# Attention with the transposes three heads behind, VectorE normalising first, and negated logits

## The reference

```
logits = where(valid, (q @ k.T) * SCALE + bias, NEG)
m = max(max(logits), sink)                  # sink: first 16 heads alone
e = exp(logits - m)
p = e / (sum(e) + exp(sink - m))
y = p @ v                                   # 256 x 64 per head
yn = rms(y[:, :1024]) * ga ++ rms(y[:, 1024:]) * gb
x = x + g1 * (yn @ w_o)
x = x + g2 * experts(rms(x) * (1 + sc2) + sh2)
```

## Time and profile before

| | us |
|---|---|
| median of 3 runs | 1583.15 |
| lowest, highest | 1582.28, 1590.99 |
| profiled execution | 1584.59 |
| its span | 1582.8 |
| PE busy, share | 1361.7, 86% |
| DVE busy, share | 652.2, 41% |
| ACT busy, share | 138.7, 9% |
| first scores of the attention | 307.78 |
| last square sum ends | about 402.9 |

### The profile page before, as it was taken

One profiled execution on the slowest core, in us unless ns is written; L12 is line 12 of the kernel. 1 busy time (PEld: TensorE's weight loads), 2 busy tenths in 40 slices (PEclk: granted clock), 3 DMA queues, 4 the chain that ended last, 5 costly groups with the idle time before them and its releaser, 6 DMA issues.

```text
span 1582.8 us, 14568 instructions
## 1 busy us (share of the span) xinstructions
PE 1361.7 (86%) x5720; PEld 690.4 (44%) x5720; DVE 652.2 (41%) x984; ACT 138.7 (9%) x390; POOL 48.2 (3%) x60
## 2 busy tenths in 40 slices
PE   2799998898898468998988988988988988988985
PEld 2678777566687355332332322332332332332321
DVE  4557676556575632224224224223223223233234
ACT  2110000146200011000000000000000000000001
POOL 0000000000100000000000000000000000000000
PEclk9899999959999789999999999999999999999998
DMA  9999999814498860999999999999999999999992
GB/s 334 397 361 401 394 362 359 323 69 160 141 392 324 314 266 27 376 425 428 424 426 429 424 425 430 424 425 429 424 425 429 424 425 430 424 425 430 424 424 85
DMA packets 96295, 572.10 MB, mean 361 GB/s; under 512 B 6048, under 2 KB 28752, under 8 KB 54400
## 3 DMA queue, kind: packets, MB, share of 16 engines
q1 hardware_dynamic: 94256, 567.64, 87.8%
q0 software_dynamic: 2000, 3.95, 0.9%
HBM read 569.38 MB, written 2.18 MB: 361 GB/s over the span
## 4 chain that ended last, share of the span: by engine, by line
PE 65%; DMA 24%; DVE 6%; issue 3%; ACT 1%; SPq 1%; DVEq 0%; POOL 0%; POOLq 0%; ACTq 0%
PE PS L1298 20%; DMA ring<-in_w_up 18%; PE PS L1319 10%; PE PS L1144 9%; PE PS L1278 8%; PE PS L1223 5%; PE PS L1149 3%; DMA ring<-in_w_ada 3%; DMA ring<-in_w_o 2%; PE PS L1260 2%; DVE W L761 2%; DVE W L1029 1%; PE PS L1094 1%; PE PS L1174 1%; PE PS L1194 1%
## 5 line engine op out<-in xcount | busy, mean ns | idle before, releaser
L1298 PE MATMUL PS<-ring,W 128*64 128x512 f32 x1024 | 239.0, 624 | 38.3 <-DMA ring<-in_w_up 38.1
L1319 PE MATMUL PS<-ring,W 128*64 128x512 f32 x1024 | 233.6, 610 | 27.4 <-DVE W L1029 17.7
L1298 PE MATMUL PS<-ring,gysq 128*64 128x512 f32 x1024 | 229.4, 604 | 15.9 <-DMA ring<-in_w_up 12.4
L1144 PE MATMUL PS<-r,ring 128*128 128x256 f32 x768 | 171.2, 386 | 9.2 <-DVE r L771 7.5
L1007 DVE TENSOR_TENSOR r<-r,PS 128x512 f32<-128x512 f32 x128 | 88.0, 688 | 200.5 <-PE PS L1278 200.5
L1298 PEld LDWEIGHTS PS<-ring,W 128*64 128x64 f32 x1024 | 81.2, 144 | 190.4 <-issue 190.4
L1144 PEld LDWEIGHTS PS<-r,ring 128*128 128x128 f32 x768 | 148.5, 194 | 32.6 <-DVE r L771 8.3
L761 DVE SCALAR_TENSOR_TENSOR W<-ring,sm,W 128x2048 f32<-128x2048 f32 x60 | 140.8, 2347 | 40.4 <-DMA ring<-in_w_ada 37.2
L1012 DVE TENSOR_SCALAR W<-W 128x256 f32<-128x256 f32 x32 | 22.0, 689 | 311.5 <-ACT W L660 311.5
L1298 PEld LDWEIGHTS PS<-ring,gysq 128*64 128x64 f32 x1024 | 78.6, 139 | 164.6 <-issue 164.6
L1319 PEld LDWEIGHTS PS<-ring,W 128*64 128x64 f32 x1024 | 76.2, 140 | 163.6 <-issue 144.0
(11 more groups left out here) (207 smaller groups left out, 737.3 us busy)
## 6 DMA issues: line engine op xcount, KB each, us to landing
ring<-in_w_gate SPq DMA_DIRECT2D x64, 2048.0 KB, 25.2
ring<-in_w_up SPq DMA_DIRECT2D x64, 2048.0 KB, 27.0
ring<-in_w_down SPq DMA_DIRECT2D x64, 2048.0 KB, 26.2
ring<-in_w_ada SPq DMA_DIRECT2D x32, 2048.0 KB, 15.4
ring<-in_w_qkv SPq DMA_DIRECT2D x17, 2048.0 KB, 16.7
ring<-in_w_ada SPq DMA_DIRECT2D x32, 1024.0 KB, 14.3
ring<-in_w_o SPq DMA_DIRECT2D x8, 2048.0 KB, 14.7
ring<-u_scr SPq DMA_DIRECT2D x2, 2048.0 KB, 19.8
```

Source lines behind the costliest of these rows:

```text
L1144: last = mm(ps[:, sub * T:(sub + 1) * T], w[:, t, (2 * b + sub) * P:(2 * b + sub + 1) * P], hT[:, QT * q + t, :], start=(t == 0), stop=(t ...
L1298: last = mm(PS[64 * j:64 * j + 64, i % 2, :].rearrange("p (m n) -> p m n", m=2), hE[i % 2][:, k], w[:, :, t, 256 * j:256 * j + 256], start ...
L1319: last = mm(PS[64 * q:64 * q + 64, 4 + i2, :], hidT[:, b, 64 * j:64 * j + 64], w[:, b, 512 * ch:512 * ch + 512], start=(j + b == 0), stop= ...
```

## The change

Logits are kept negated: q is scaled by -SCALE and the bias table is negated, so that the row minimum of the negated logits is the negated maximum that Exp needs as its bias, and Exp runs with scale -1. L840 goes. DVE normalises head h-2 first, then evicts y, and takes logits(h) last. Transposes run three heads behind, values and everything behind them two steps later; a fifth buffer for logits is added. The squares are no longer summed over blocks on PE: ACT writes the first block's square of each half into `ysq`, POOL adds each further one, and two products with ones follow after the loop. The waits for the modulation row move: ACT's behind head 3, PE's behind the loop, and POOL does its adds between the write of row SH2 and its read back.

```diff
-    line[rel_bucket(dist), np.arange(UL)] = (dist >= 0)
+    line[rel_bucket(dist), np.arange(UL)] = -1.0 * (dist >= 0)
...
+        ysq = gy
+        Ls = [L[:, i] for i in range(4)] + [W[:, 2816:2816 + 384]]
+        NL = len(Ls)
...
+            def add_square(b):                                   # POOL
+                i, n = divmod(b, KT // 2)
+                if n:
+                    pool.wait_ge(sq_ok, b + 1)
+                    total = ysq[:, i * T:(i + 1) * T]
+                    nc.gpsimd.tensor_tensor(total, total, sq[:, b % 2 * T:(b % 2 + 1) * T], ALU.add).then_inc(ysq_ok, 1)
+                    pool.wait_ge(ysq_ok, b - i)
...
                 pool.dma_start(m_scr[pt_].rearrange("(q n) -> q n", q=4), rows).then_inc(mod_out, 16)
+                if pt_ == SH2:
+                    for h in range(NH + 7):
+                        if h >= 8 and h % 2 == 0:
+                            add_square((h - 8) // 2)
                 pool.wait_ge(mod_out, 16 * (i + 1))
...
             def exps(h):                                         # ACT
-                act.wait_ge(nm_ok, h + 1)
-                A.activation(L[:, h % 4, 0:T], L[:, h % 4, 0:T], ACT.Exp, bias=nmx[:, h, 0:1],
+                act.wait_ge(lg_ok, h + 1)
+                Lh = Ls[h % NL]
+                A.activation(Lh[:, 0:T], Lh[:, 0:T], ACT.Exp, bias=nmx[:, h, 0:1], scale=-1.0,
                              accum_out=psum_[:, h, 0:1])
...
             def squares(b):
                 act.wait_ge(y_ok, b + 1)
-                if b >= 2:
-                    act.wait_ge(yss_ps, b - 1)
-                A.activation(sq[:, b % 2 * T:(b % 2 + 1) * T], yT[:, b, :], ACT.Square).then_inc(sq_ok, 1)
-            act.wait_ge(mod_out, 16 * 2)
+                i, n = divmod(b, KT // 2)
+                if n == 0:
+                    A.activation(ysq[:, i * T:(i + 1) * T], yT[:, b, :], ACT.Square).then_inc(sq_ok, 1)
+                else:
+                    if b >= 3:
+                        act.wait_ge(ysq_ok, b - 2 - (b - 2) // (KT // 2))
+                    A.activation(sq[:, b % 2 * T:(b % 2 + 1) * T], yT[:, b, :], ACT.Square).then_inc(sq_ok, 1)
             act.wait_ge(small_in, 32)
-            for h in range(NH + 4):
+            for h in range(NH + 7):
                 if h < NH:
                     exps(h)
-                if 2 <= h < NH + 2:
-                    pt_evac(h - 2)
-                if h >= 5 and h % 2 == 1:
-                    squares((h - 5) // 2)
+                if h == 3:
+                    act.wait_ge(mod_out, 16 * 2)
+                if 3 <= h < NH + 3:
+                    pt_evac(h - 3)
+                if h >= 8 and h % 2 == 0:
+                    squares((h - 8) // 2)
...
+            link(V.tensor_scalar(nsink, sink, -1.0, None, ALU.mult))      # DVE
             def logits(h):
                 dve.wait_ge(s_ps, h + 1)
-                if h >= 4:
-                    dve.wait_ge(pt_ps, h - 3)
+                if h >= NL:
+                    dve.wait_ge(pt_ps, h - NL + 1)
...
-                dve.wait_ge(lg_ok, h + 1)
-                V.tensor_scalar(nmx[:, h, :], nmx[:, h, :], -1.0, None, ALU.mult).then_inc(nm_ok, 1)
...
-            for h in range(NH + 4):
-                if h < NH:
-                    logits(h)
-                if 1 <= h <= NH:
-                    normalise(h - 1)
-                if h >= 5 and h % 2 == 1:
-                    y_evac((h - 5) // 2)
-            dve.wait_ge(yss_ps, NH // 2)
+            for h in range(NH + 6):
+                if 2 <= h < NH + 2:
+                    normalise(h - 2)
+                if h >= 7 and h % 2 == 1:
+                    y_evac((h - 7) // 2)
+                if h < NH:
+                    logits(h)
+            dve.wait_ge(yss_ps, 2)
...
-            pe.wait_ge(mod_ok, 2)                                # PE
-            for h in range(NH + 5):
+            for h in range(NH + 6):
                 if h < NH:
                     scores(h)
-                if 2 <= h < NH + 2:
-                    transpose_p(h - 2)
-                if 4 <= h < NH + 4 and h % 2 == 0:
-                    values((h - 4) // 2)
+                if 3 <= h < NH + 3:
+                    transpose_p(h - 3)
                 if h >= 6 and h % 2 == 0:
-                    square_sums((h - 6) // 2)
+                    values((h - 6) // 2)
+            pe.wait_ge(mod_ok, 2)
+            for i in range(2):
+                pe.wait_ge(sq_ok, KT // 2 * i + 1)
+                pe.wait_ge(ysq_ok, (KT // 2 - 1) * (i + 1))
+                mm(PS[:, 6 + i, 0:T], ones, ysq[:, i * T:(i + 1) * T], start=True, stop=True).then_inc(yss_ps, 1)
```

More of the change, by code:

```diff
@@ L39 @@
 NEG = -1e30
-LOW = -3.0e38
+HIGH = 3.0e38
 SCALE = 1.0 / math.sqrt(HD)
@@ L102, in constants @@
     line = np.zeros((BUCKETS, 2 * UL), np.float32)
-    line[rel_bucket(dist), np.arange(UL)] = (dist >= 0)
+    line[rel_bucket(dist), np.arange(UL)] = -1.0 * (dist >= 0)
     bad = np.zeros((NH, UL), np.float32)
-    bad[:NHA, (dist < 0) | (dist >= WINDOW)] = NEG
-    bad[NHA:, dist < 0] = NEG
+    bad[:NHA, (dist < 0) | (dist >= WINDOW)] = -NEG
+    bad[NHA:, dist < 0] = -NEG
     line[:, UL:] = bad
@@ L184, in layer_kernel @@
         gy, sq = gysq[:, 0:H * CW], gysq[:, H * CW:H * CW + 2 * T]
+        ysq = gy
         idr = sb("idr", H * P)
-        sm = sb("sm", 608)
+        sm = sb("sm", 624)
         ovi = sb("ovi", 1, I32)
@@ L248, in small @@
             at[0] += n
-            assert at[0] <= 608
+            assert at[0] <= 624
             return sm[:, at[0] - n:at[0]]
@@ L256, in layer_kernel @@
         A1, B1, A2, B2 = small(KT), small(KT), small(KT), small(KT)
-        sink = small(NHA)
+        sink, nsink = small(NHA), small(NHA)
         nmx, psum_, rden = (small(NH * 2).rearrange("p (h t) -> p h t", t=2) for _ in range(3))
@@ L301, in layer_kernel @@
         qkv_ok = sem("qkv_ok")
-        s_ps, lg_ok, nm_ok, p_ok, sum_ok = sem("s_ps"), sem("lg_ok"), sem("nm_ok"), sem("p_ok"), sem("sum_ok")
+        s_ps, lg_ok, p_ok, ysq_ok = sem("s_ps"), sem("lg_ok"), sem("p_ok"), sem("ysq_ok")
         pn_ok, pt_ps, pt_ok, y_ps, y_ok, sq_ok, yss_ps = (sem("pn_ok"), sem("pt_ps"), sem("pt_ok"), sem("y_ps"),
@@ L561, in _ @@
                     if k < 2:
-                        A.activation(query(k, b), backwards(ps), ACT.Copy, scale=SCALE).then_inc(qkv_ok, 1)
+                        A.activation(query(k, b), backwards(ps), ACT.Copy, scale=-SCALE).then_inc(qkv_ok, 1)
                     elif k == 2:
@@ L578, in exps @@
             def exps(h):
-                act.wait_ge(nm_ok, h + 1)
-                A.activation(L[:, h % 4, 0:T], L[:, h % 4, 0:T], ACT.Exp, bias=nmx[:, h, 0:1],
+                act.wait_ge(lg_ok, h + 1)
+                Lh = Ls[h % NL]
+                A.activation(Lh[:, 0:T], Lh[:, 0:T], ACT.Exp, bias=nmx[:, h, 0:1], scale=-1.0,
                              accum_out=psum_[:, h, 0:1])
-                last = A.activation(L[:, h % 4, T:384], L[:, h % 4, T:384], ACT.Exp, bias=nmx[:, h, 1:2],
+                last = A.activation(Lh[:, T:384], Lh[:, T:384], ACT.Exp, bias=nmx[:, h, 1:2], scale=-1.0,
                                     accum_out=psum_[:, h, 1:2])
@@ L770, in add_part @@
                 if k < 2:
-                    V.scalar_tensor_tensor(query(k, b), backwards(ps), SCALE, query(k, b), ALU.mult,
+                    V.scalar_tensor_tensor(query(k, b), backwards(ps), -SCALE, query(k, b), ALU.mult,
                                            ALU.add).then_inc(qkv_ok, 1)
@@ L826, in _ @@
             mod_row(1)
+            dve.wait_ge(small_in, 32)
+            link(V.tensor_scalar(nsink, sink, -1.0, None, ALU.mult))
             def logits(h):
                 dve.wait_ge(s_ps, h + 1)
-                if h >= 4:
-                    dve.wait_ge(pt_ps, h - 3)
+                if h >= NL:
+                    dve.wait_ge(pt_ps, h - NL + 1)
                 B = on_ring(dve, "bias", h // 16).rearrange("p (h k) -> p h k", h=16)[:, h % 16, :]
[L834 to L838, removed]
-                dve.wait_ge(lg_ok, h + 1)
-                V.tensor_scalar(nmx[:, h, :], nmx[:, h, :], -1.0, None, ALU.mult).then_inc(nm_ok, 1)
+                high = nsink[:, h:h + 1] if h < NHA else HIGH
+                Lh = Ls[h % NL]
+                V.tensor_tensor_reduce(out=Lh[:, 0:T], in0=PS[:, h % 2, 0:T], in1=B, scale=1.0, scalar=high,
+                                       op0=ALU.add, op1=ALU.min, accum_out=nmx[:, h, 0:1])
+                V.tensor_tensor_reduce(out=Lh[:, T:384], in0=PS[:, h % 2, T:384], in1=B[:, P:T], scale=1.0,
+                                       scalar=high, op0=ALU.add, op1=ALU.min, accum_out=nmx[:, h, 1:2]).then_inc(lg_ok, 1)
             def normalise(h):
                 dve.wait_ge(p_ok, h + 1)
+                Lh = Ls[h % NL]
                 if h < NHA:
@@ L846, in normalise @@
                 link(V.reciprocal(rden[:, h, :], psum_[:, h, :]))
```

(30 more changed lines are left out.)

## The result

Median of 9 runs: 1591.66 us (1587.77 to 1592.83) against 1583.89 before (1579.11 to 1590.99). The ratio is 1.0047, 95% interval 1.0027 to 1.0066. The profiled execution took 1588.92 (span 1587.1), 4.3 above the profiled one of before; it is the second fastest of the nine.

The account below looks back on a forecast made before the run. Attention was taken as the bound, PE alone at 1.2 GHz and a three-engine round at full clock. Start, loop and tail gave +7.8, tail clock -1.6, w_o -0.3: +5.9, 1589 us as median, range 1571 to 1595.

Parts of the forecast that it names:

- Fall at 311: Start of attention: PE's thin stretch lets the clock fall to 0.50 at 311 us or one step later.
- No rise in the loop: Attention loop: without the full-array square sums PE stays at 1.2 GHz through the whole loop; 59 in 100.
- rival A: Attention: full clock returns at about 322 once PE is filled; L864 at 374, -29, total 1554; 6 in 100.
- Start, -1.8: Start of attention: ACT's wait for m_scr moves behind head 3, so first transposes come 1.8 us earlier, at about 313.2.
- Loop, 94.5 us of PE work, pair 6.30: Attention loop at 1.2 GHz: PE alone sets 6.30 us per pair, 94.5 us left, last values end at 407.7.
- Tail: Last values to L864: 3.0 us instead of 1.7, with POOL's last add; clock returning there gives back 1.6.
- The clock came back in the tail: After scores 31: 7.8 us of dense transposes and values bring the clock back, -1.6 (0 to -2.8).
- the bounds: Tail: POOL's last two-input add takes between 0.26 and 2.1 us, with 0.8 taken.
- w_o, -0.3: Start of w_o after attention: begins at the lower clock again, slow work slightly shorter, -0.3 (-1 to +0.5).
- The total: Whole kernel: terms sum to +5.9, 1590.5 us in the profiled frame, 1589 in that of the median.
- 1.90 us per head: First 16 heads at full clock: DVE's logits, normalise and half an eviction take 1.90, or 3.8 per pair.

Follow-up runs that it names:

- experiment 1: Kernel after, with PE multiplying constants (seven fillers) in its waits in the first seven steps: 1556.33 us, ratio 0.9828.
- experiment 2: Kernel before, with the same kind of fillers where PE waits at the start: 1575.10 us, ratio 0.9961.
- experiment 3: Kernel after, with one burst of four 512-column products behind scores 12 and no other filler: 1569.43 us, ratio 0.9896.
- experiment 4: Kernel after with the ramp fillers of experiment 1, without those behind scores 4 to 6: 1590.06, 1587.69, 1588.47 and 1556.35 us.
- experiment 5: Kernel after, with one 256-column full-array filler behind each pair's values: 1563.36 us, ratio 0.9886.
- experiment 6: Kernel before, with only its square sums moved from PE to POOL: 1600.25 us, ratio 1.0108.
- experiment 7: Kernel after, with square sums back on PE, no POOL adds, and PE's modulation-row wait ahead of the loop: 1602.22 us, ratio 1.0116.
- experiment 8: As experiment 7, with each square sum issued two steps later so PE finds its square ready: 1574.61 us, ratio 0.9933.
- experiment 10: As experiment 8, with fillers in the ramp and in the gap before w_o: 1558.71 us, ratio 0.9859.

## Why the prediction was right, step by step

- **Fall at 311.** Right: 311.6. Experiments 1 and 2 show that the thin ramp causes it. The moment itself moves: in the profiled executions of experiments 3 to 8 without fillers in the ramp it was 308.2 to 311.4.
- **No rise in the loop.** Right: 0.50 until 403.8. The reason given, that the loop lost the product which made its densest stretch, is borne out by 6 (that part alone keeps the clock down), by 5 and 8 (a full-array product in the same place brings the rise back), and in part by 7, where the product is there but a wait splits the stretch, and the clock rises only at 392.6. The Trainium skill's rule (TensorE: Matmul & The Clock Gate, Why this matters) that PE kept busy without idle gaps runs at full speed would have given rival A; the rows of experiment 4 speak against it as plainly as those of the kernel after, 85.20 busy of 85.20 us at 0.50. The prediction also said that the rise would be still less likely if transposes did not count as busy. They do count: just before the rise at 403.8 PE did transposes for half of the time (1.47 against 1.48 of values, from 400.69), and in the loop, which did not rise, for a quarter (1.66 of 6.30). If they counted for nothing, the tail would be thinner than the loop.

```profile
400.69 1.47 PE PS L1209 x6
402.17 1.48 PE PS L1221 x12
```

- **Start, -1.8.** Measured -1.8 (5.40 against 7.20).
- **Loop, 94.5 us of PE work, pair 6.30.** The pair is right. From the first transposes to the end of the last scores I counted 86.7 (94.5 less the 7.8 of the tail); it took 313.99 to 400.62, 86.6.
- **Tail.** I had 9.2 from there to the mean squares (7.8 + 3.0 - 1.6); it took 408.79 - 400.62 = 8.2. The clock came back in the tail as forecast, and gave more than I took: the last transposes and values took 5.4 instead of 7.8 (400.62 to 406.05), the last product 0.7 instead of 1.15. The add took 0.73, between the bounds and near the 0.8 taken. The Trainium skill (GPSIMD Engine Reference, 4.1 Engine selection) puts two-input work on POOL at about twice DVE's time, from which the prediction estimated 0.7; the trace agrees, 0.73 against half of the 0.69 that DVE's 128x512 add takes.
- **w_o, -0.3.** It was -1.4 up to the experts; 0.9 of it is the first three chunks (43.27 against 44.16).
- **The total.** +5.9 forecast, +4.3 between the two profiled executions, +7.8 between the medians. That the sum fits so well is partly luck: tail and w_o were each about 1 too high, and the start of the stage, 0.8 later, was not in it. The median of before seems to move with the moment of the rise, which only one of its executions shows directly: in the 13 runs beside experiments 8 and 10 the fastest had a mean clock of 0.945 and 1577.0 us, the slowest 0.933 and 1593.97. The kernel after has no such moment, and its runs lie 5.1 us apart.

Of the parts at the full clock I had DVE too slow: 1.90 us per head, counted with the hand-overs of before. Experiment 1 passes a pair in 3.46. It changed nothing at the lower clock, but rival A was 1.5 us too high by it (nine heads at 1.90 instead of 1.73).

## What to carry to other kernels

Read the granted clock of a stage before its busy times: here, at the lower clock, PE alone was the chain of the loop, the edits that relieved another engine there were worth nothing, and the one that thinned PE's own stream cost more than it saved. Where a pipeline fills slowly, try letting PE multiply constants in its waits until the loop runs; here seven such products were worth 35 us in the kernel after, and nine were worth 9 us in the kernel before. And try a change at both clocks, or its worth is that of the state it happened to meet.

## What the runs showed of the hardware

- A loop can be stable at both clocks: 34 us at 0.50 and 44 us at 1.00 on either side of one burst (experiment 3).
- A PE that is busy without a gap for 85 us can stay at the lower clock (experiment 4). In this loop the scores use 64 of 128 rows and the values 64 of 128 columns; only the transposes use the whole array. With one full-array product more per pair, and PE just as busy, the clock rises (47.00 of 47.00 us before it in experiment 5).
- A wait for a square in front of each square sum, 0.43 us at the lower clock and 1.15 at the upper, goes with a late rise, a fall 6.8 us later and 28 us more (experiments 7 and 8).
- A two-input POOL add of 128x256 float32 takes 0.73 us (14 of them, 10.2 us in all). They can slow DVE: its L875, which reads and writes SBUF alone, takes 0.35 us. In experiment 1 ten of the 32 ran at the same time as an add, and seven of these took 0.48 to 0.87; none of the other 22 took more than 0.36. In the kernel after none ran beside an add, and none took more than 0.36.

```profile
L875 DVE TENSOR_SCALAR W<-W,sm x32: 352/353/867, 313.9 to 365.8; 128x256 f32<-128x256 f32 x32
L875 DVE TENSOR_SCALAR W<-W,sm x32: 352/353/355, 313.4 to 402.6; 128x256 f32<-128x256 f32 x32
```

The first line is experiment 1, the second the kernel after: number, shortest, median and longest in ns.

What stays open: whether it is the used part of the array that counts. Every added product used the whole array; none used half of it, for as long. Open too is at which pair the clock rises in the kernels that can rise. It differs from run to run (1561 to 1578 us in experiment 5), and experiments 5 and 8, with nearly the same PE stream, have medians 11 us apart.
